# A transformer block and a mixture-of-experts block on one core: the first gather from tokens' own positions, a modulation piece in the norms, a tail in another order, expert weights by halves

## What is computed

```python
mod = silu(c) @ w_ada + b_ada                      # six rows of 1024: sh1 sc1 gt1 sh2 sc2 gt2
h = rms_norm(x, g_pre_mix) * (1 + sc1) + sh1
mix = concat(diff_attention(h), neighbourhood_attention(h)) @ w_out
x = x + gt1 * rms_norm(mix, g_post_mix)
h2 = rms_norm(x, g_pre_ffn) * (1 + sc2) + sh2
logits = h2 @ w_router + b_router                  # 32 experts, top 4 per token
gates = softmax(top4(logits))
f = sum over the 4 experts e of a token:  gate * (swiglu(h2 @ w1[e] + b1[e]) @ w2[e] + b2[e])
out = x + gt2 * rms_norm(f, g_post_ffn)
```

## Time and profile before

| | us |
|---|---|
| median of 3 runs | 1462.79 (1462.68 to 1463.17) |
| the profiled execution | 1464.81 |
| its span | 1463.0 |
| TensorE busy | 1318.0 (90%) |
| VectorE busy | 533.2 (36%) |
| ScalarE busy | 400.8 (27%) |
| moved by the DMA | 508.74 MB, mean 348 GB/s |
| mean granted TensorE clock | 0.977 |

### The profile page before, as it was taken

How to read it: one execution, slowest core, us unless ns; L and a number is a source line. 1 busy time by engine, 2 the same in 40 slices (tenths; PEclk the granted TensorE clock), 3 DMA queues, 4 the chain that set the end, 5 groups by cost and what they waited for, 6 DMA issues and landing times.

```text
span 1463.0 us, 32870 instructions
## 1 busy us (share of the span) xinstructions
PE 1318.0 (90%) x13170; PEld 792.2 (54%) x13170; DVE 533.2 (36%) x1088; ACT 400.8 (27%) x744; POOL 0.2 (0%) x4
## 2 busy tenths in 40 slices
PE   9999999999999989899999899877997879978796
PEld 8998689997688653343434334323442324333242
DVE  6843668884597751112111121111211211111122
ACT  6734445542456641111111111011110111111111
POOL 0000000000000000000000000000000000000000
PEclk9999999999999989999999999999999999999998
DMA  8431985544863589999999999999999999999995
GB/s 362 174 116 59 402 328 198 197 191 172 297 278 116 224 365 385 428 428 427 427 427 427 428 427 427 426 428 429 427 426 427 428 428 427 425 428 428 429 426 217
DMA packets 36383, 508.74 MB, mean 348 GB/s; under 512 B 4064, under 2 KB 4192, under 8 KB 5472
## 3 DMA queue, kind: packets, MB, share of 16 engines
q1 hardware_dynamic: 36288, 507.34, 83.3%
HBM read 506.28 MB, written 1.05 MB: 347 GB/s over the span
## 4 chain that ended last, share of the span: by engine, by line
PE 62%; DMA 25%; ACT 5%; DVE 5%; issue 3%; SPq 0%; DVEq 0%; ACTq 0%
PE acc L1275 19%; DMA low<-in_w 16%; PE acc L506 9%; PE acc L1292 8%; DMA high_part<-in_w 7%; PE acc L1265 3%; PE acc L1250 3%; PE acc L969 2%; PE acc L1007 2%; PE acc L544 2%; DMA low<-in_stream 2%; PE acc L1257 1%; PE acc L545 1%; ACT high_part L1876 1%; PE acc L889 1%
## 5 line engine op out<-in xcount | busy, mean ns | idle before, releaser
L1275 PE MATMUL acc<-low,high_part 128*32 128x512 f32 x2384 | 284.3, 605 | 46.3 <-DMA low<-in_w 32.7
L2457 DVE TENSOR_SCALAR high_part<-acc 128x256 f32<-128x256 f32 x53 | 22.5, 425 | 514.4 <-PE acc L1275 514.4
L1275 PEld LDWEIGHTS acc<-low,high_part 128*32 128x32 f32 x2384 | 83.8, 111 | 203.6 <-issue 145.5
L1292 PE MATMUL acc<-low,high_part 128*32 128x256 f32 x2624 | 155.4, 387 | 8.3 <-DMA low<-in_w 8.3
L1874 ACT ACTIVATE high_part<-high_part 128x256 f32<-128x256 f32 x53 | 22.1, 417 | 470.5 <-DVE high_part L2457 470.5
L1460 DVE TENSOR_TENSOR w_lo<-low,w_hi 128x4096 fp32r<-128x4096 f32 (+1 forms) x30 | 130.5, 4353 | 35.8 <-ACT w_hi L1454 35.4
L1275 PE MATMUL acc<-high_part 128*32 128x512 f32 x1008 | 121.1, 607 | 22.0 <-DMA high_part<-in_w 18.5
L1292 PEld LDWEIGHTS acc<-low,high_part 128*32 128x32 f32 x2624 | 81.7, 111 | 74.4 <-DMA low<-in_w 11.2
L1454 ACT ACTIVATE w_hi<-low 128x4096 fp32r<-128x4096 f32 (+1 forms) x28 | 99.8, 3568 | 52.5 <-DMA low<-in_stream 43.0
L1265 PE MATMUL acc<-high_part 32*128 32x256 f32 x864 | 78.7, 433 | 14.4 <-ACT high_part L1891 11.5
L1275 PEld LDWEIGHTS acc<-high_part 128*32 128x32 f32 x1008 | 36.9, 111 | 90.8 <-issue 60.8
(11 more groups left out here) (497 smaller groups left out, 1810.2 us busy)
## 6 DMA issues: line engine op xcount, KB each, us to landing
low<-in_w SPq DMA_DIRECT2D x141, 2048.0 KB, 35.7
high_part<-in_w SPq DMA_DIRECT2D x51, 2048.0 KB, 34.2
low<-in_stream SPq DMA_DIRECT2D x41, 2048.0 KB, 8.0
high_part<-in_stream SPq DMA_DIRECT2D x4, 2048.0 KB, 12.1
high_part<-in_natb SPq DMA_DIRECT2D x1, 2048.0 KB, 13.3
high_part<-in_rows SPq DMA_DIRECT2D x1, 1536.0 KB, 14.0
high_part<-in_x SPq DMA_DIRECT2D x2, 512.0 KB, 4.5
low<-in_stream SPq DMA_DIRECT2D x1, 1024.0 KB, 5.5
```

Source lines behind the costliest of these rows:

```text
L1275: last = mm(flat[32 * q:32 * q + 32, 2048:2560], XG[:, b, 32 * kk:32 * kk + 32], wp[:, 2048 * b + 512 * q:2048 * b + 512 * q + 512], start ...
L1292: last = mm(flat[32 * q:32 * q + 32, 2816:3072], AT[:, 128 * (c % 2) + 32 * (c // 2):128 * (c % 2) + 32 * (c // 2) + 32], wp[:, 1024 * (c ...
L2457: ts(GLU, flat[:, 2048:2304], 7.0, None, ALU.min).then_inc(S("glu"), 1)
```

## The change

- **Modulation.** `ada(11)` follows `ada(10)`, ahead of `in2_hi(0)`. `picks` and `gate_rows` for the third group move behind the output product, among the fillers; VectorE's part moves too, the columns ahead of the norm's inverses, G2B ahead of the logits.
- **First gather.** `select(0)` no longer reads PP: SEL is made from PM, the token's position in its own expert, scaled by 1/32, when that position is known. PP is now a product less the pass's number, in units of 1/32, without RM. The gates' softmax, the products with them and the four with B2 move behind `ups(0)` (`gates`). B2 is loaded as 128 x 512 instead of 128 x 1024 and earlier. Both transposes for H2R stand together. Fillers stand at three places of the routing.
- **Constants.** `rank` moves ahead of `upto`, so that `slot_of(9)` overlies what the routing does not need; its piece is issued at the logits and the one of `slot_of(8)` after it.
- **Halves.** Every expert piece is loaded as two DMAs of 128 x 2048 (rows of 8 KB), each with its own semaphore, waited for and released on its own.
- **Tail.** `down1` of the last turn has two fillers ahead of its last two blocks; `by_gate(3)` comes first instead of last, and ScalarE's fourth square waits for it.

```diff
-               ("upto", P), ("same", P), ... ("window", 64), ("rank", 2 * NE + 8)):
+               ("rank", 2 * NE + 8), ("upto", P), ("same", P), ... ("window", 64)):
+NROUTING = CO["upto"][0]
...
+            def expert_half(e, n, half, signal):
+                r = EXPERT_PIECES[n][1]
+                src = w1[bass.ds(4 * e + r, 1), :, half] if r < 4 else w2[bass.ds(2 * e + r - 4, 1), :, half]
+                sp.dma_start(slot_of(n)[:, half], src.rearrange("a p n -> (a p) n")).then_inc(S(signal), 16)
             def expert_piece(e, n):
-                sp.dma_start(slot_of(n), src.rearrange("a p n -> (a p) n"))\
-                  .then_inc(S(f"slot{n % NSLOT}_loaded"), 16)
+                expert_half(e, n, HALF_A, f"slot{n % NSLOT}_loaded")
+                expert_half(e, n, HALF_B, f"slot{n % NSLOT}_rest")
...
             expert_piece(0, 4)
+            sp.dma_start(B2, b2).then_inc(S("b_in"), 16)
...
-            sp.wait_ge(S("x4"), 2 * T)
-            sp.wait_ge(S("b1_parts"), B1PARTS)
-            sp.dma_start(B2, b2).then_inc(S("b_in"), 16)
+            sp.wait_ge(S("logits"), 1)
+            expert_piece(1, NLOW + 1)
             sp.wait_ge(S("h2r"), T)
             expert_piece(1, NLOW)
-            sp.wait_ge(*step("pp"))
-            expert_piece(1, NLOW + 1)
...
-            def released(last, r):
-                if r < 3:
-                    sp.wait_ge(S("wused"), 3 * last + r + 1)
-                else:
-                    sp.wait_ge(S(("w1", "w2_half", "w2")[r - 3]), last + 1)
+            def released(last, r, h):
+                if r < 3 or (r == 3 and h == 0):
+                    sp.wait_ge(S("wused"), 7 * last + 2 * r + h + 1)
+                elif r == 3:
+                    sp.wait_ge(S("w1"), last + 1)
+                elif r == 4 or h == 0:
+                    sp.wait_ge(S("w2_part"), 3 * last + 2 * (r - 4) + h + 1)
+                else:
+                    sp.wait_ge(S("w2"), last + 1)
...
             pe_norm(3)
             ada(10)
+            ada(11)
...
             in2_hi(0, 0, 4)
-            ada(11)
             in2_lo(0, 0, 4)
             in2_hi(1, 0, 2)
-            pe.wait_ge(S("modr"), 3)
-            picks(2, 1).then_inc(*signal("modc2"))
-            gate_rows(1, 2)
...
             out_lo(1, 1)
-            keep_busy(7, 6, NLASTING)
+            pe.wait_ge(S("modr"), 3)
+            pe.wait_ge(S("by_gate"), 2)
+            picks(2, 5).then_inc(*signal("modc2"))
+            keep_busy(7, 3, NLASTING)
+            gate_rows(1, 6)
             pe_norm_by_tile()
...
+            pe.wait_ge(S("h2r_in"), 1)
+            keep_busy(0, 1, NLASTING)
+            pe.wait_ge(S("pm"), 1)
+            for t in range(T):
+                last = nc.tensor.transpose(flat[0:32, 3840 + 128 * t:...], PM[:, t, :], ident)
+            last.then_inc(*signal("pmt"))
+            keep_busy(0, 1, NLASTING)
             pe.wait_ge(*step("cnr"))
...
+            pe.wait_ge(S("sel"), 1)
+            pe.wait_ge(S("h2r_in"), 2)
+            gather()
             pe.wait_ge(*step("perm"))
...
+            gather_transpose()
+            pe.wait_ge(S("oh"), 1)
             for t in range(T):
-                mm(flat[:, o:o + NPMAX], PMT[0:32, ...], OH[0:32], start=True, stop=False)
-                last = mm(flat[:, o:o + NPMAX], ones[0:32, :], RM[0:32], start=False, stop=True)
+                last = mm(flat[:, o:o + NPMAX], PMT[0:32, ...], OH[0:32], start=True, stop=True)
             last.then_inc(*signal("pp"))
+            keep_busy(1, 1, NLASTING)
...
             def up1(loaded):
                 for kk in range(4):
-                    wp = loaded(kk)
                     for b in range(2):
+                        wp = loaded(kk, b)
...
-                    if kk < 3:
-                        last.then_inc(S("wused"), 1)
+                        if 2 * kk + b < 7:
+                            last.then_inc(S("wused"), 1)
...
-            def down1(loaded):
+            def down1(loaded, busy):
                 for c in range(KC):
-                    if c % 4 == 0:
-                        wp = loaded(4 + c // 4)
+                    if busy and c == 6:
+                        keep_busy(4, 2, NLASTING)
+                    if c % 2 == 0:
+                        wp = loaded(4 + c // 4, c // 2 % 2)
...
+            def gates():
+                pe.wait_ge(S("gate"), 1)
...
             ups(0, first, turns)
+            gates()
             downs(0, first, turns, first + turns)
...
+            v.wait_ge(*step("modc2"))
+            moved(5, 0, 2, 24)
+            link(stt(GW2, MODC[:, 24:32], 1.0, vec("pre_ffn"), ALU.add, ALU.mult))
             for t in range(T):
                 v.wait_ge(S("ssq"), squares_4 + 2 * t + 2)
                 inverse(t)
...
+            v.wait_ge(S("gtb"), 2)
+            tt(G2B, G2B, bank(6, 2), ALU.mult).then_inc(S("gtb_in"), 1)
             v.wait_ge(*step("lg"))
...
-            ts(PM, PM, 1000.0, None, ALU.add).then_inc(S("gate"), 1)
+            ts(PM, PM, 1000.0, 1.0 / CAP, ALU.add, ALU.mult).then_inc(S("pm"), 1)
...
+            for t in range(T):
+                last = ts(SEL[:, t, :], slot[:, 0:CAP], PM[:, t, 0:1], None, ALU.is_equal)
+            last.then_inc(S("sel"), 1)
             v.wait_ge(*step("cnr"))
...
             downs(NE - 1, ATALL)
+            v.wait_ge(S("scat"), ... + 1)
+            by_gate(3, (0, 1, 2, 3), G2B)
             for i in range(3):
...
-            by_gate(3, (0, 1, 2, 3), G2B)
             v.wait_ge(S("rstd"), ROOTS.index("e") + 1)
```

More of the change, by code:

```diff
@@ L59 @@
 for _n, _w in (("ident", P), ("ones", P), ("slot", P), ("before", P), ("count", NPMAX),
-               ("upto", P), ("same", P), ("after", P), ("level", 6 * GCH), ("eye", GCH), ("later", GCH),
-               ("dist", 2 * L), ("window", 64), ("rank", 2 * NE + 8)):
+               ("rank", 2 * NE + 8), ("upto", P), ("same", P), ("after", P), ("level", 6 * GCH), ("eye", GCH), ("later", GCH),
+               ("dist", 2 * L), ("window", 64)):
     CO[_n] = (_at, _w)
@@ L271, in first_block_and_moe @@
         SG, SGT = three(temp(256), T), temp(256)
-        PP, GP = (three(at(CST + NLASTING + NPIECE + T * NPMAX * i, T * NPMAX), T) for i in range(2))
-        assert CST + NLASTING + NPIECE + 2 * T * NPMAX <= BC + 2048
+        PP, GP = (three(at(CST + CO[name][0], T * NPMAX), T) for name in ("before", "count"))
+        assert CO["count"][0] + T * NPMAX <= NROUTING and CST + NROUTING + NPIECE <= BC + 2048
         OH, OHB = at(A8_AT, NPMAX), at(A8_AT + NPMAX, CAP // 2).bitcast(BF16)
@@ L434, in _ @@
                     e, of_expert = expert_in_turn(turn), turn
-                released(last, r)
-                expert_piece(e, n)
+                released(last, r, 0)
+                expert_half(e, n, HALF_A, f"slot{n % NSLOT}_loaded")
+                released(last, r, 1)
+                expert_half(e, n, HALF_B, f"slot{n % NSLOT}_rest")
             for t in range(T):
@@ L1200, in _ @@
             last.then_inc(S("h2r"), 1)
-            keep_busy(7, 2, NLASTING)
+            for k in range(KC):
+                last = nc.tensor.transpose(flat[:, 1024 + 128 * k:1024 + 128 * k + 128], HT[:, k, 128:256], ident)
+            last.then_inc(S("h2r"), 1)
+            pe.wait_ge(S("gtb_in"), 2)
             pe.wait_ge(*step("mask"))
@@ L1313, in up_pass, with down_pass @@
                 last.then_inc(S("at"), 1)
-            def down_pass(p, made, loaded):
+            def down_pass(p, made, loaded, busy):
                 pe.wait_ge(S("y_in"), p + 1)
@@ L1328, in down_pass @@
                 pe.wait_ge(S("at_in"), p + 1)
-                down1(loaded)
-            pe.wait_ge(S("sel"), 1)
-            pe.wait_ge(S("h2r_in"), 2)
-            gather()
-            pe.wait_ge(S("g_in"), 1)
-            gather_transpose()
-            pe.wait_ge(S("b_in"), 16)
-            for q in range(4):
-                t, h = divmod(q, 2)
-                r = slice(32 * q, 32 * q + 32)
-                mm(bank(q), GTT[r, 128 * t:128 * t + 128], B2[r, 512 * h:512 * h + 512], start=True, stop=False, skip_group_check=True)\
-                  .then_inc(S("b2_in"), 1)
+                down1(loaded, busy)
+            def gates():
+                pe.wait_ge(S("gate"), 1)
+                for t in range(T):
+                    last = mm(flat[:, 512 + 128 * t:512 + 128 * t + 128], GATE4[:, t, :], ident, start=True, stop=True)
+                last.then_inc(*signal("gtp"))
+                pe.wait_ge(*step("gtt_in"))
+                for t in range(T):
+                    o = 2560 + NPMAX * t
+                    last = mm(flat[:, o:o + NPMAX], GTT[0:32, 128 * t:128 * t + 128], OH[0:32], start=True, stop=True)
+                last.then_inc(*signal("gp"))
+                pe.wait_ge(S("b_in"), 16)
+                for q in range(4):
+                    r = slice(32 * q, 32 * q + 32)
```

(15 more changed lines are left out.)

118 lines of the change are left out of this document (52 added, 66 removed).

## The result

The kernel after takes 1466.41 us (median of 9 runs), the kernel before beside it 1462.79 us (9 runs): 3.6 us more; ratio 1.0026, 95% interval 1.0016 to 1.0036. The forecast was 1457.8 us, faster. The profiled execution of after took 1467.5 us with a span of 1465.8; that of before 1464.8 and 1463.0. The spans differ by 2.8 us, and that is the amount the traces can explain.

A forecast was written before the change was run, and what follows sets the result against it. The expert weight stream, 181 pieces at full DMA rate, was taken to bound the kernel. The span 1463.0 - 10.3 (start) + 8 (small rows) - 2.7 (tail) = 1458.0 us gave 1457.8 us as the median, range 1450.0 to 1465.5.

The forecast's parts named there:

- Part 1: Modulation piece moved into TensorE's wait in the attention stage: all that follows 2.5 us earlier, the norm 0.3 us longer.
- Part 2: Routing's first gather from its own positions: gather 4.5 us sooner, first up product 5.8 us sooner on its own.
- The rival in which TensorE stays at 1.2 GHz through the gather: Start of the expert stream gains only half, 6.0 instead of 10.3 us: 1462.1 us, chance 0.18.
- Part 3, start: Half-buffer releases and the earlier first product: expert weight stream starts 10.3 us earlier, first refill at 540.2 us.
- Part 3, surcharge: Expert weight stream with 8 KB instead of 16 KB rows: 8 us longer over 181 pieces.
- the slower rival: Expert stream: small rows cost as the 4 KB rows do, 21 us against gains of 13.0: 1470.7 us, chance 0.08.
- Part 4: Tail: 16 instead of 32 matmuls after the last byte, and gate product moved: 2.7 us saved together.
- TensorE as the new bound: After the restart, moved gate work and earlier stream eat the backlog near 686 us: about 1463.8 us, chance 0.04.
- Free packets: Expert stream: small packets cost nothing, the DMA rate being held by something else: 1449.8 us, chance 0.15.
- A fixed price for each transfer: Expert stream: each of 181 added transfers costs its start, another 8 us: 1465.8 us, chance 0.02.

The follow-up runs named there:

- halves at both ends: The kernel after with halves only for the first four refills and the last piece, whole pieces in between; 1452.14 us, ratio 0.9923 against before.

## Why the forecast was wrong, step by step

- **Part 1** (2.5 us, bounds 1.4 to 4.4): right. In after the stage's end is 3.0 us earlier (482.83 against 485.82); alone it gives 2.65 us there, 2.1 us at the first product and 1.6 to 1.9 us of time. From there to the first product 0.5 us are lost, where the forecast put 0.3 on the norm.
- **Part 2** (5.8 us): right in the total, 5.8 us between the two kernels with and without it, and in the gather's start (4.5 forecast, 4.75 measured). From the gather to the first product the forecast had 1.3 us from the work moved and none from the clock; it was 1.0 us, and 0.9 of it are the clock's, so that the total agrees is partly luck. First product forecast 538.7, measured 538.18 us. The rival in which TensorE stays at 1.2 GHz through the gather did not happen.
- **Part 3, start** (10.3 us): 9.6 us, first refill at 539.46 against 540.2. But the early half release, one reason for the change, could not be seen: whole pieces with all else kept land as early as halves at both ends.
- **Part 3, surcharge** (8 us): 15.0 us, and **this is the step that failed**. The term was mis-sized: the rows alone cost 13.7 us over 181 pieces (8 KB rows in one transfer), 75 ns a piece instead of 44; with the second transfer it is 14.6 us over the 176 pieces in which after and the halves at both ends differ, 83 ns a piece, by their last landings. The forecast named 9 ns a row and 72 ns a piece as the point from which the slower rival decides, and the price is past it. The rival's own size, 15 ns a row, was too high.
- **Part 4** (2.7 us): 2.7 us from the first matmul (14.9 to 12.2 us). Its reason is only partly right: with the modulation move alone, TensorE waited 2.82 us for the last piece and then needed 1.93 us for the 32 matmuls, not the 3.34 us of the earlier trace rows. The clock's 1.4 us are not lost in every execution, and the comparison of two spans had this in it.
- **The other rivals.** TensorE as the new bound: in after it still waits 62.5 us for DMA between 600 and 1440 us, and whole pieces alone bring 427 GB/s back, so no. Free packets: no, the rate fell. A fixed price for each transfer: 7 ns, not 44.

What failed was how the price was read. The forecast took both packet times from stretches where the queue was otherwise quiet, 611 and 309 ns, called the 7 ns between them the nearest price, and went down from it (9.6 us to 8) for an overlap of packets. Upward it had only the 15 ns of the 4 KB rows, with a chance of 0.08. In the loaded stream the queue rows above give other times. Before: (12,800 x 1.003 - 2,606 x 0.009) / 20,823 = 615 ns for 16 KB. After: (12,800 x 1.010 - 5,128 x 0.010) / 41,021 = 314 ns for 8 KB. (The numerators are the 16 engines' 12,800 us in 800, by the queue's share, less the 4-byte packets, the semaphore writes, of 9 to 10 ns.) A packet of either size takes 4 to 5 ns more in the loaded stream than in the quiet one, so twice as many packets pay it twice: 2 x 314 - 615 = 13 ns a row. The part of the shares above 100%, packets that overlap, is 6 ns for two small ones and 2 for a large one, which leaves 9 ns, the price that the landings show. The 615 ns stood in the trace of before, beside the 611. With them, and with the same 4 ns given to the small packet, which no row of before shows, the forecast would have been 2 x (309 + 4) - 615 = 11 ns a row, 16 us over the stream, and the sum 1449.8 + 16 = 1465.8 us, slower than before. The step that failed is that a price from the quiet stretches was carried into the loaded stream, and lowered. Why a packet takes longer under load is open.

The Trainium skill, DMA: Bandwidth & Descriptors, section Why small descriptors are slow, puts about 3 cycles on a packet, an estimate of 3.5 ns at its 850 MHz. The runs here show 8.8 to 9.7 ns for each packet from 4 to 32 KB; the trace does not agree. With that estimate the surcharge would have been 5 us instead of 8, and the forecast 3 us further from the result.

## What to carry to other kernels

Where a stream of weights keeps all DMA engines busy, the number of packets costs time beside the bytes: here about 9 ns for each packet on each engine, so halving the rows of 888 us of stream costs more than a finer release can give back. Split a transfer only where its latency is on the path (here the last piece; halves for the first refills brought nothing that could be seen), or split it so that the rows stay long; and price a packet in the loaded stream, never in a quiet stretch. When the chain of waits suddenly names the issuing queue, ask first whether the rate behind it has fallen.

## What was not expected of the hardware

- The price of a packet hardly depended on its size over a factor of eight: 9.3, 9.4 and 9.7 ns for each packet more or less at 4, 8 and 32 KB, each from single executions and good to about half a ns. The number of transfers hardly counted (7 ns each on an engine).
- The 16 engines drift apart by 9.6 us (before) and 12.0 us (after) in 890 us of equal shares, in both traces as seven early and nine late ones, and from 1440 us on before runs at 226 GB/s and less. At 1400 us 18.2 MB are left in before and 19.5 MB in after, at full rate enough until 1442.6 and 1446.3 us; the last packets end 5.0 and 6.7 us later, so the taper costs after 1.7 us more. What sets the order of the engines is open.
- Eight neighbouring rows to a transfer halved the rate of all engines, 203 GB/s at a share of 1.02.
- The granted clock held at 2.4 GHz through 1.38 us of waiting ahead of the last matmuls and fell in the scatter behind them (0.63 from 1440 to 1441 us, then 0.50); the same 2.8 us wait was followed by 3.34 us for 32 matmuls in one execution (before) and by 1.93 us in another (the modulation move alone).
